# Joining the stops that turn modulation sums into columns, in a one-core fp32 diffusion backbone kernel

## What is computed

```python
sc = jax.nn.silu(c)
scc = jax.nn.silu(c_ctx)
for i in range(DEPTH):                      # DEPTH = 2
    mod_l = sc @ ada_w[i] + ada_b[i]        # (1024) @ (1024, 6144)
    sh1, s1, g1, sh2, s2, g2 = jnp.split(mod_l[:, None, :], 6, axis=-1)
    mod_c = scc @ ada_w[i] + ada_b[i]
    ...
    h_l = x * (1.0 + s1) + sh1
    ...
    x = _layernorm(DN_ALPHA * x + g1 * y_l, ln1_g[i], ln1_b[i])
    x = _layernorm(DN_ALPHA * x + g2 * _sq_relu_mlp(x * (1.0 + s2) + sh2, ffn_w1[i], ffn_w2[i]),
                   ln2_g[i], ln2_b[i])
```

## Time and profile before

| | before |
|---|---|
| time, median of 3 runs | 1923.31 us |
| time of the profiled execution | 1922.92 us |
| its span (first to last instruction) | 1921.1 us |
| PE busy | 1912.0 us (100% of the span) |
| VectorE busy | 1401.8 us (73%) |
| ScalarE busy | 671.6 us (35%) |
| mean share of the DMA engines in stretches from 885 to 902 us | 0.99 to 1.11 |

### The profile page before, as it was taken

The page is one execution under the profiler, slowest core; times in us unless marked ns, Lnnn a source line. Parts: engine busy times, 40 slices in busy tenths (PEclk is TensorE's granted clock), DMA queues, the critical chain, the costliest instruction groups (busy, mean ns, idle before and its releaser), DMA issues.

```text
span 1921.1 us, 24854 instructions
## 1 busy us (share of the span) xinstructions
PE 1912.0 (100%) x9399; PEld 1648.1 (86%) x9399; DVE 1401.8 (73%) x2023; ACT 671.6 (35%) x927; POOL 382.3 (20%) x364
## 2 busy tenths in 40 slices
PE   9999999999999999999999999999999999999998
PEld 7889899899889988999888888888888888888887
DVE  3766588798898887878887755744764787767778
ACT  3423122245323322332536325324423444434443
POOL 0300311313221222212410120030030037100004
PEclk9999999999999999999999999999999999999999
DMA  9623334335998999998696285366447435977656
GB/s 336 259 68 72 117 121 133 119 122 143 209 238 211 223 233 227 235 247 214 178 240 243 68 271 174 109 213 197 150 158 213 165 105 168 244 212 192 178 148 145
DMA packets 120424, 350.63 MB, mean 183 GB/s; under 512 B 17520, under 2 KB 30448, under 8 KB 115568
## 3 DMA queue, kind: packets, MB, share of 16 engines
q1 hardware_dynamic: 91200, 268.11, 41.0%
q0 software_dynamic: 27280, 77.08, 22.2%
q10 hardware_dynamic: 1824, 3.85, 0.6%
HBM read 296.01 MB, written 40.92 MB: 175 GB/s over the span
## 4 chain that ended last, share of the span: by engine, by line
PE 98%; DMA 1%; POOL 1%; issue 0%; SPq 0%; ACT 0%; POOLq 0%; DVE 0%; ACTq 0%; DVEq 0%
PE bank L1171 18%; PE bank L1173 18%; PE bank L1172 18%; PE bank L1211 4%; PE bank L1209 4%; PE bank L1210 4%; PE bank L1580 4%; PE bank L1581 4%; PE bank L1578 4%; PE bank L1627 3%; PE bank L1628 3%; PE bank L1625 3%; PE bank L1810 2%; PE bank L1809 2%; PE bank L1807 2%; PE bank L1487 1%
## 5 line engine op out<-in xcount | busy, mean ns | idle before, releaser
L2375 DVE TENSOR_TENSOR w_lo<-raw,w_hi 128x1024 fp32r<-128x1024 f32 x132 | 167.7, 1274 | 152.7 <-ACT w_hi L1833 152.5
L1833 ACT ACTIVATE w_hi<-raw 128x1024 fp32r<-128x1024 f32 x132 | 139.3, 1055 | 275.1 <-PE bank L1173 156.3
L1171 PE MATMUL bank<-w_hi,act_hi 128*128 128x512 f32 x504 | 197.4, 392 | 0.0
L1173 PE MATMUL bank<-w_hi,act_lo 128*128 128x512 f32 x504 | 196.4, 390 | 0.0
L1172 PE MATMUL bank<-w_lo,act_hi 128*128 128x512 f32 x504 | 196.3, 389 | 0.0
L1171 PE MATMUL bank<-hT_hi,w_hi 128*128 128x384 f32 (+2 forms) x544 | 191.8, 353 | 0.0
L1172 PE MATMUL bank<-hT_lo,w_hi 128*128 128x384 f32 (+2 forms) x544 | 190.8, 351 | 0.0
L1173 PE MATMUL bank<-hT_hi,w_lo 128*128 128x384 f32 (+2 forms) x544 | 190.8, 351 | 0.0
L1209 PE MATMUL bank<-w_hi,hT_hi 128*128 128x512 f32 x336 | 130.9, 390 | 0.0
L1210 PE MATMUL bank<-w_lo,hT_hi 128*128 128x512 f32 x336 | 130.8, 389 | 0.0
L1211 PE MATMUL bank<-w_hi,hT_lo 128*128 128x512 f32 x336 | 130.7, 389 | 0.0
(11 more groups left out here) (462 smaller groups left out, 4854.2 us busy)
## 6 DMA issues: line engine op xcount, KB each, us to landing
raw<-w_units_d SPq DMA_DIRECT2D x234, 512.0 KB, 4.6
mod<-mod_units_d SPq DMA_DIRECT2D x64, 384.0 KB, 5.0
wsum<-w_units_d SPq DMA_DIRECT2D x44, 512.0 KB, 4.5
raw<-weight_sums_d SPq DMA_DIRECT2D x32, 512.0 KB, 4.3
wsum<-w_units_d POOLq DMA_DIRECT2D x25, 512.0 KB, 7.5
wsum<-wsum POOLq DMA_DIRECT2D x19, 512.0 KB, 6.9
bv<-mod_units_d SPq DMA_DIRECT2D x16, 512.0 KB, 3.5
weight_sums_d<-w_units_d POOLq DMA_DIRECT2D x8, 1024.0 KB, 14.0
```

Of the source, the lines that this page charges most:

```text
L1171: nc.tensor.matmul(out, s_hi, m_hi, start=first, stop=False)
L1173: return nc.tensor.matmul(out, s_lo, m_hi, start=False, stop=last)
L1833: nc.scalar.activation(halves_of(phase, k, i)[0], raw[:, s, :], ACT.Copy).then_inc(hi_done, 1)
L2375: tt(lo, raw[:, s, :], f32(hi), ALU.subtract).then_inc(lo_done, 1)
```

## The change

Three things change.

- The `cols0` stops are joined. In the gMLP the two stops become one, in its third piece (32 columns wide in place of 16 twice). In the first MLP six stops become two: one at p = 2 for groups 0 to 2 (36 columns), and one in `ffn0z` for groups 3 to 7 (30 columns). The partial sums of all groups wait in `part_sums`, which is wider now.
- Groups 6 and 7 of the second network are summed by VectorE, as the others are: group 6 in the down-projection of p = 5, between the drains; group 7 in `ffn0z`, right behind its last `mod_product`. PE's `rows0` step of `ffn0z` and ACT's copy of it are gone, and PE's transposes there give way to the joined `cols0`.
- Where a stop is gone, the step before it counts for two in `pe_step` and `dve_drain`, so that later counts stay as they are.

```diff
-    if phase in ("ln0a", "ln0b"):
+    if phase == "ln0a":
         out += _ROWS
...
+        JOINS1 = {PIECES_MIXED - 1: (0, 2, PIECES_MIXED), PIECES_F - 2: (PIECES_MIXED, 1, PIECES_F - PIECES_MIXED)}
...
                                 if q == 1:
-                                    last.then_inc(pe_step, 1)
+                                    last.then_inc(pe_step, 2 if t == after and half == 1 and joined else 1)
...
-            def part_columns(phase, i, label, n, vectors):
+            def part_columns(phase, i, label, n, vectors, groups=1):
...
                 for q in range(4):
-                    src = sums[:, 0:vectors, 0:4 * n].rearrange("p v (j q) -> p q j v", q=4)[:, q]
-                    last = nc.tensor.matmul(bank[7][32 * q:32 * q + 32, 0:n * vectors].rearrange("p (j v) -> p j v", v=vectors),
+                    w = groups * vectors * n
+                    src = sums[:, 0:4 * w].rearrange("p (g v j q) -> p q g j v", v=vectors, j=n, q=4)[:, q]
+                    last = nc.tensor.matmul(bank[7][32 * q:32 * q + 32, 0:w].rearrange("p (g j v) -> p g j v", v=vectors, j=n),
                                             sel32, src, start=True, stop=True, tile_position=(0, 32 * q))
...
-                def rows():
-                    pe.wait_ge(mod_used, len(MOD1_SEQ))
-                    mod_sums(phase, i, "rows0", 6, [sum1(p), sum1(PIECES_F - 1, 1)], WIDE_M1 // 2)
-
                 def columns():
-                    mod_columns(phase, i, 0, rows1, 7)
+                    part_columns(phase, i, "cols0", 6, *JOINS1[p][1:3])
...
-                    down_blocks(phase, 7, LN_ORDER["ln0b"], act_hi0, act_lo0, ready, "ln0b", rows=rows,
-                                columns=columns)
+                    down_blocks(phase, 7, LN_ORDER["ln0b"], act_hi0, act_lo0, ready, "ln0b", columns=columns)
...
-                    act.wait_ge(dve_drain, drained("ffn0", p - 1, "cols0")[1])
-                    mod_rows(phase, i, 0, rows1[:, :], 6, begin)
...
+                def later_sum(n):
+
+                    if p == PIECES_F - 3:
+                        group1_sum(PIECES_F - 2, n - 2)
+                    else:
+                        group1_sum(p, n)
...
                 products(1)
+                if phase == "ffn0z":
+                    group1_sum(PIECES_F - 1, 0)
+                    group1_sum(PIECES_F - 1, 1)
                 less_common(0)
                 less_common(1)
                 block0_lo(p, 4)
```

More of the change, by code:

```diff
@@ L1216, in token_units, with down @@
                             between[q, t]()
-            def down(phase, i, k0, tiles, a_hi, a_lo, ready, late=None, columns1=None, after=1):
+            def down(phase, i, k0, tiles, a_hi, a_lo, ready, late=None, columns1=None, after=1, joined=False):
                 for half in range(2):
@@ L1549, in _ @@
                     down(phase, i, CH, TILES0, act_hi0, act_lo0, ready,
-                         columns1=lambda: part_columns(phase, i, "cols0", 8, 2))
+                         columns1=(lambda: part_columns(phase, i, "cols0", 8, 2, PIECES_A - 2)) if p == PIECES_A - 2 else None,
+                         joined=p < PIECES_A - 2)
                 else:
@@ L1596, in ffn0 @@
                     down(phase, i, 7, TILES0, act_hi0, act_lo0, ready, after=TILES0 - 2,
-                         columns1=lambda: part_columns(phase, i, "cols0", 6, 2 if p < PIECES_MIXED else 1))
-                else:
-                    down_blocks(phase, 7, LN_ORDER["ln0b"], act_hi0, act_lo0, ready, "ln0b", rows=rows,
-                                columns=columns)
+                         columns1=(lambda: part_columns(phase, i, "cols0", 6, *JOINS1[p][1:3])) if p in JOINS1 else None,
+                         joined=p not in JOINS1)
+                else:
+                    down_blocks(phase, 7, LN_ORDER["ln0b"], act_hi0, act_lo0, ready, "ln0b", columns=columns)
             ffn0a()
@@ L2476, in ln_split, with drain @@
                             behind[m]()
-            def drain(phase, i, half, t, tiles):
+            def drain(phase, i, half, t, tiles, steps=1):
                 e = BASE[phase]["add"] + half * tiles + t
@@ L2506, in block0_lo, with drain0 @@
                 tt(lo, src, f32(hi), ALU.subtract).then_inc(lo_done, 1)
-            def drain0(p, half, t):
+            def drain0(p, half, t, steps=1):
                 phase, i = piece0(p) if p >= 0 else ("ffn0a", 0)
@@ L2615, in ffn0 @@
                     drain0(p, 1, 0)
-                    group1_sum(p, 2)
+                    later_sum(2)
                     drain0(p, 1, 1)
-                    group1_sum(p, 3)
+                    later_sum(3)
                     for t in range(2, TILES0 - 1):
-                        drain0(p, 1, t)
+                        drain0(p, 1, t, 2 if t == TILES0 - 2 and p not in JOINS1 else 1)
                         products(5, t - 2)
-                    add_part_bias(phase, i, "cols0", 1, 6 * i, 6, 2 if p < PIECES_MIXED else 1)
+                    if p in JOINS1:
+                        g, vectors, groups = JOINS1[p]
+                        add_part_bias(phase, i, "cols0", 1, 6 * g, 6 * groups, vectors)
                     block0_lo(p + 1, 1)
@@ L2652, in down @@
                 for t in range(tiles):
-                    drain(phase, i, 1, t, tiles)
+                    drain(phase, i, 1, t, tiles, 2 if t == 1 and sums and not columns else 1)
                     if t == 1 and columns:
@@ L2923, in product, with part_sum @@
                 last.then_inc(used, 1)
-            def part_sum(done, v, a, src, turned, sums=part_sums):
+            def part_sum(done, at, src, turned, sums=part_sums):
                 n = src.shape[1] // 32
@@ L3117, in group1_sum @@
                 w = WIDE_M1 // 2
[L3118 to L3127 removed]
+                at = 24 * (2 * p + v if p < PIECES_MIXED else p - PIECES_MIXED) + half * w // 32
+                part_sum(sums_made("ffn0", p) - 4 * vectors + 2 * n, at, sum1(p, v)[:, half * w:(half + 1) * w], rows1[:, :])
             def gate_unit(k):
```

34 lines of the change are left out of this document (15 added, 19 removed).

## The result

| | before | after |
|---|---|---|
| median of 22 runs | 1923.18 us | 1926.62 us |
| lowest and highest | 1922.51 to 1926.56 | 1925.38 to 1927.54 |
| profiled execution, its span | 1922.92, 1921.1 us | 1926.50, 1924.7 us |

The ratio is 1.0017 with a 95% interval of 1.0011 to 1.0024: 3.4 us slower, within the 0.2% that I had called no change, but 4.5 us above the predicted time and outside the range. In the tables of experiments "ratio" means the same.

What follows compares the result with a forecast made beforehand. The prediction took PE to bound the kernel (busy 1912.0 of 1921.1 us). PE's saving of 3.25 us less 2.00 lost to group 7's sums gave -1.25, so 1922.1 us from a median of 1923.31; range 1920.0 to 1924.1.

Steps and rivals of the forecast that it cites:

- What PE saves, 3.25 us: gMLP, first MLP and `ffn0z`: removed stops, `rows0` and transposes give 4.60 us, three joined stops take back 1.35.
- The 0.60 us a stop in the range: Upper bound for each joined stop's cost to PE, from 0.41 to 0.60 us; the forecast used 0.45.
- Group 6's sums, cost nothing: Down-projection of p = 5: VectorE's added 2.33 us is taken up by waits of 1.05 and 1.64 us.
- Group 7's sums, 2.00 us of PE: `ffn0z`, ahead of product 4: sums push VectorE by 2.33 us against 0.50 margin; PE loses 2.00, bounds 1.9 to 2.1.
- its 2.4 us in seven: PE's weight-load waits with VectorE as releaser, read as few and short: VectorE delivers in time.
- SP's queue has the same entries in the same order: Claim on SP's load queue after the change; the forecast gave it no cost.
- the case: The main forecast: PE saves 3.25 us, loses 2.00 in `ffn0z`, giving 1922.1 us (1921.8 to 1922.8); chance 0.5.
- the slice with 0.2 us of margin: Load for group 7's third product in `ffn0z`: issued at 897.3, landed at 902.0, needed at 902.20 us.
- The rival of the late load: Group 7's last products in `ffn0z`: group 6's sums delay the load's issue, VectorE waits; 1922.8 to 1924.3 us, chance 0.22.
- A DMA that is full all the time finishes them when it did: Argument against the late load before group 7's last product: same bytes, mostly same times, so unchanged landings.
- so I count no recovery: Behind the stall ahead of product 4 in `ffn0z`: VectorE stays 2.33 us late and PE 2.00.
- The sum: Whole kernel: -3.25 + 2.00 = -1.25 us, added to the median 1923.31, gives 1922.1 us.

Runs made afterwards that it cites:

- the kernel with the early product: The changed kernel with product 59 moved from `ffn0z` to the end of p = 5, so the last load is issued earlier: 1922.80 us, ratio 1.0001 to the kernel before.
- the add held back: The changed kernel with GpSimd's 512 KB accumulating transfer issued only once the last slice (63) has landed: 1923.45 us, ratio 1.0003 to the kernel before.

## Why the prediction failed, step by step

- **What PE saves, 3.25 us.** Right where PE doesn't meet another engine. PE saved 2.50 us ahead of `ffn0z` and 0.91 in it, 3.41 in all. The joined stop was put at 0.45; it is 33.16 - 32.68 = 0.48 at p = 2 and 0.42 in `ffn0z`. The Trainium skill, "TensorE: Matmul & The Clock Gate", section "Back-to-back issue gap", gives a floor of 25 ns for a matmul of this width, which makes an estimate of 0.20 us for eight; the trace doesn't agree for these either. I left out one margin: ACT's first half of the last token tile ended some 0.27 us ahead of PE's transposes in the kernel before (947.22 + 1.52 / 2 = 947.98, PE at 948.25). So the 0.9 us of `rows0` and the transposes is PE's only if PE comes late, as it does in the changed kernel. Where PE is on time, it waits there (0.38 to 1.21 us in five kernels, all without `rows0`). The 0.60 us a stop in the range had no row behind it, and no run shows it (0.48 at most); the range's upper end was added up to -0.5 where its terms give -0.6, which changes nothing.
- **Group 6's sums, cost nothing.** PE has no wait there: product 1 to product 3 of `ffn0z` start at their usual distance. Whether they are the reason that GpSimd's add came ahead of the load is open. With them moved to `ffn0z` the load came first in one kernel (0.55 us ahead) and the add in the other (1.94 us).
- **Group 7's sums, 2.00 us of PE.** Right but for 0.15: 2.03 of wait and 0.12 behind it in the kernel with the early product. There the last product ends at 901.12, the first transpose starts at 901.15 and `less_common` at 903.51, where it would have started at 901.03 without the chain: a push of 2.48 us and not 2.33, since the first transpose did not start ahead of its predecessor's end. One reading of the earlier trace rows was too short: its 2.4 us in seven are one group of waits for VectorE in the retention mixer, and the list has five more rows of VectorE, 2.2 us together. In the stretch from 860 to 950 us only one of them stands, 0.6 us.
- **"SP's queue has the same entries in the same order."** This is the step that failed, by 2.81 us: the case put a late load at nothing. The sentence is true, and it was the wrong question: the landing of this load depended on what GpSimd's queue had in flight too. The earlier trace rows show landings of 4.7 to 6.9 us, and I took the fastest one for granted, for the slice with 0.2 us of margin. The rival of the late load had the right place and mechanism, with 0.22; its price was too low. I took 6.9 us as the slowest; 7.7 came, and VectorE waited 2.89 us. "A DMA that is full all the time finishes them when it did" is refuted: with GpSimd's add issued first the load took 6.5 to 7.7 us, with it behind 4.1 to 4.7. The Trainium skill, "DMA: Bandwidth & Descriptors", section "SWDGE vs HWDGE vs iDMA", says that queues of both kinds feed the same DMA engines, which take turns between them; the runs agree, since the add held back took 3.1 us off the landing.
- **The stall priced at its own length ("so I count no recovery").** The second step that failed. Behind the wait, PE worked at a granted clock of about one half until 912.7 us and lost another 2.20 us. No case of mine had it.
- **The sum.** -1.25 was forecast. The late load adds 4.81 - 2.00 = 2.81 and the clock 2.20, which gives +3.76; PE saved 0.16 more than forecast, which gives the +3.6 of the spans.

What stays open: why the clock fell behind waits of 2.02 and 2.60 us, and not behind 2.03, 2.29 and 1.80. From 3.23 us up it fell each time (3.23, 3.99, 4.42, 4.81). Each of these nine is one profiled execution, and since the size of the fall seems to differ between executions of one kernel, the shorter waits may fall in some and not in others; no run here shows it. Open too are what puts GpSimd's add ahead of the load, and why the early loads took 6.3 to 6.8 us with the 512 KB behind them.

## What to carry to other kernels

When work is added to an engine, look for its next instruction that waits for a transfer, and give that load more margin than the spread of the landings of its kind, other queues' transfers included; here three microseconds' earlier issue (one product moved) turned 1926.6 into 1922.8. Price a stall of PE of 2 us or more with a bound for the clock behind it, 0 to about 3 us here, and not by its length alone. A stop taken out of PE's stream pays only up to the next place where another engine's chain arrives: read that margin before counting the saving, also far behind the change.

## What the runs showed of the hardware

- A stop of four matmuls on 32-column tiles costs PE 0.41 us with 6 or 12 columns and 0.48 with 36, by the length of a down-projection with it and without. Read at the stop itself it is 0.38 with 6 or 12 columns (887.97 - 887.13 - 0.46), 0.39 with 16, 0.42 with 30 and 0.45 with 36.
- A load of 384 KB through SP's queue lands in 4.1 to 4.7 us where GpSimd's accumulating transfer of 512 KB is issued behind it (four kernels), and in 6.5 to 7.7 us where that is issued 0.6 to 1.9 us ahead (four kernels). That holds for the load at 894.8 to 897.6 us; issued at 891.3 to 891.8, with the 512 KB 2.3 us or more behind it, it took 6.3 to 6.8 us (five kernels).
- Behind PE waits of 3.2 to 4.8 us the granted clock was 0.50 to 0.66 in a window of 5 us; matmuls of 384 columns stood 0.32 us apart in place of 0.17, and the product behind took 5.61 to 7.05 us in place of 4.16. Behind waits of 2.02 and 2.60 us it fell too (5.84 and 5.86 us); behind 1.80, 2.03 and 2.29 it stayed at 1.00.
